# Dense products of a two-block float32 transformer kernel: 512-column matmuls over the high and low parts of x side by side

## The reference

```python
proj = xn @ w_in                                   # 2048 -> 8272
h = h + concat([y_h, y_a]) @ w_out                 # 2048 -> 2048
h = h + square(relu(rms_norm(h) @ w_up)) @ w_down  # 2048 -> 8192 -> 2048
q = rmsnorm(h) @ a_w_in                            # 2048 -> 4096, pooled and gated
h = h + y @ w_out_2                                # twice
```

## Time and profile before

| | |
|---|---|
| median of 3 runs | 2654.34 us (2654.14 to 2654.96) |
| the profiled execution | 2653.12 us |
| its span, first to last instruction | 2651.3 us |
| PE busy | 2428.7 us, 92% |
| POOL busy | 2059.1 us, 78% |
| ACT busy | 1059.0 us, 40% |
| DVE busy | 926.5 us, 35% |
| HBM traffic | 150 GB/s over the span |

### The profile page before, as it was taken

The page is one execution under the profiler, slowest core; times in us unless marked ns, Lnnn a source line. Parts: engine busy times, 40 slices in busy tenths (PEclk is TensorE's granted clock), DMA queues, the critical chain, the costliest instruction groups (busy, mean ns, idle before and its releaser), DMA issues.

```text
span 2651.3 us, 45198 instructions
## 1 busy us (share of the span) xinstructions
PE 2428.7 (92%) x18299; PEld 2322.7 (88%) x18299; DVE 926.5 (35%) x1484; ACT 1059.0 (40%) x1282; POOL 2059.1 (78%) x1956
## 2 busy tenths in 40 slices
PE   6999998868997899999999999998899977999996
PEld 6989997657996799999999999998899956988896
DVE  5026661635252353021031131605514043055522
ACT  3344444474334333333333333433434323244532
POOL 6988984655785679899899999799687958665583
PEclk9999998998998999999999999999999978899998
DMA  5654433332443345555555555454354535433241
GB/s 178 194 169 145 143 105 120 134 140 98 159 159 111 124 137 185 188 177 187 179 182 184 180 185 192 153 187 148 122 187 149 193 109 174 133 110 111 97 157 50
DMA packets 206437, 400.30 MB, mean 151 GB/s; under 512 B 10434, under 2 KB 20932, under 8 KB 205252
## 3 DMA queue, kind: packets, MB, share of 16 engines
q1 hardware_dynamic: 206276, 397.99, 46.1%
HBM read 395.87 MB, written 2.10 MB: 150 GB/s over the span
## 4 chain that ended last, share of the span: by engine, by line
PE 56%; POOL 25%; issue 8%; DVE 6%; ACT 3%; DMA 1%; POOLq 0%; SPq 0%; DVEq 0%; ACTq 0%
PE bank L579 49%; POOL w_low L546 25%; PE bank L696 1%; PE bank L779 1%; PE bank L715 1%; ACT w_high L1035 1%; PE bank L732 1%; PE bank L685 1%; DVE x_low L1473 0%; DVE x_high L1385 0%; DVE x_high L1470 0%; DMA ring<-in_w_in 0%; PE bank L942 0%; DVE heads_scratch L1803 0%; DVE proj L1329 0%
## 5 line engine op out<-in xcount | busy, mean ns | idle before, releaser
L546 POOL TENSOR_TENSOR w_low<-ring,w_high 128x512 fp32r<-128x512 f32 (+3 forms) x1888 | 2049.4, 1117 | 547.9 <-ACT w_high L1035 543.4
L1035 ACT ACTIVATE w_high<-ring 128x1024 fp32r<-128x1024 f32 (+2 forms) x760 | 788.0, 1040 | 1441.8 <-PE bank L579 1414.4
L579 PE MATMUL bank<-x_high,w_high 128*128 128x256 f32 x4196 | 1214.7, 289 | 75.4 <-DVE x_low L1389 21.4
L579 PE MATMUL bank<-x_low,w_high 128*128 128x256 f32 x4196 | 1200.5, 286 | 0.0
L579 PE MATMUL bank<-x_high,w_low 128*128 128x256 f32 x4196 | 1199.8, 286 | 0.0
L579 PEld LDWEIGHTS bank<-x_high,w_high 128*128 128x128 f32 x4196 | 819.8, 195 | 89.0 <-issue 56.3
L579 PEld LDWEIGHTS bank<-x_low,w_high 128*128 128x128 f32 x4196 | 819.8, 195 | 1.6 <-issue 1.4
L579 PEld LDWEIGHTS bank<-x_high,w_low 128*128 128x128 f32 x4196 | 818.8, 195 | 0.0
L579 PE MATMUL bank<-hidden,w_high 128*128 128x256 f32 x2048 | 368.8, 283 | 0.0
L579 PEld LDWEIGHTS bank<-hidden,w_high 128*128 128x128 f32 x2048 | 319.5, 192 | 0.0
L579 PE MATMUL bank<-hidden,w_low 128*128 128x256 f32 x1024 | 289.8, 283 | 0.0
(11 more groups left out here) (250 smaller groups left out, 1667.1 us busy)
## 6 DMA issues: line engine op xcount, KB each, us to landing
ring<-in_w_in SPq DMA_DIRECT2D x64, 1024.0 KB, 5.4
ring<-in_w_up SPq DMA_DIRECT2D x64, 1024.0 KB, 5.3
ring<-in_w_down SPq DMA_DIRECT2D x64, 1024.0 KB, 5.0
ring<-in_w_out SPq DMA_DIRECT2D x48, 1024.0 KB, 5.0
ring<-in_a_w_in SPq DMA_DIRECT2D x32, 1024.0 KB, 5.3
ring<-in_b_w_in SPq DMA_DIRECT2D x32, 1024.0 KB, 5.3
ring<-in_w_kv SPq DMA_DIRECT2D x24, 1024.0 KB, 5.1
ring<-in_w_mem_kv SPq DMA_DIRECT2D x16, 1024.0 KB, 5.0
```

The costliest lines, as they stand in the source:

```text
L546: last = pool.tensor_tensor(w_low[:, u % UNITS, part], ring[:, u // 2, first:first + n], w_high[:, u % UNITS, part], ALU.subtract)
L579: mm = pe.matmul(out, lhs, rhs, start=start and n == 0, stop=stop and n == 2, skip_group_check=True)
L1035: act.activation(w_high[:, u % UNITS, 0:n], ring[:, u // 2, r0 * g.width:r0 * g.width + n], ACT.Copy)\
```

## The change

The dense feature products hgrn_qf, mix_out, up0 to up3, down0 to down3, pool_in, out0 and out1 (4, 4, 32, 6, 4 and 4 blocks, 54 in all) are made in another way. x_high and x_low (and the two parts of hidden) lie side by side for each k tile, 512 columns. PE moves both past one load of w_high, into a bank of its own for each of the 4 feature blocks, and adds w_low times x_high with 256 columns to the first half of the bank. In each k tile the four wide matmuls come first, then the four narrow ones. A group takes four banks, 0 to 3 or 4 to 7. DVE adds the two halves of a bank when it reads it: four instructions for the second halves, a wait, four for the first halves, then the rest. The second halves go to a scratch of their own or to hT. At the first block of a product the norm's sums still use bank 4, so the second block waits for the root. Three products (mix_out, out0, out1) wait for all earlier groups before their first block. cross_out now has a pair of banks for each of its four groups.

```diff
-        x_high = sb("x_high", [P, KT, T], F32R)
-        x_low = sb("x_low", [P, KT, T], F32R)
+        x_split = sb("x_split", [P, KT, 2, T], F32R)
+        x_high, x_low = x_split[:, :, 0, :], x_split[:, :, 1, :]
...
+            def wide_unit(g, b, u, four, x, first, of, more=0):
+                pe.wait_ge(low_ready, 8 * b + u + 1 + more)
+                wh, wl = parts(u, g)
+                r0, rows = g.unit(u)
+                for k in range(rows):
+                    kt = first + r0 + k
+                    for f in range(4):
+                        pe.matmul(four[f][:, :], wh[:, k, f * P:f * P + P], x(kt), start=(kt == 0), stop=False,
+                                  skip_group_check=True)
+                    for f in range(4):
+                        mm = pe.matmul(four[f][:, 0:T], wl[:, k, f * P:f * P + P], x(kt)[:, 0:T], start=False,
+                                       stop=(kt == of - 1), skip_group_check=True)
+                mm.then_inc(units_used, 1)
...
+            def wide_product(name, x, made, ready=x_ready, sums=None):
...
+                        wide_unit(g, g.b0 + n, u, bank[4 * (n % 2):4 * (n % 2) + 4], x, 4 * (u // 2), KT, more)
+                for n in range(2):
+                    if n == 1 and sums:
+                        pe.wait_ge(norm_root, normed[0])
+                    block_of(n, 0, 0, n == 0)
...
+            def second_halves(four, read, out=None):
+                for f in range(4):
+                    b = four[f][:, T:2 * T]
+                    if out is None:
+                        last = dve.tensor_copy(second[:, f * T:f * T + T], b)
+                    else:
+                        last = dve.tensor_tensor(out(f), b, out(f), ALU.add)
+                last.then_inc(halves_read, 1)
+                dve.wait_ge(halves_read, read)
+            def first_halves(four, out=None):
+                for f in range(4):
+                    to = second[:, f * T:f * T + T] if out is None else out(f)
+                    last = dve.tensor_tensor(to, four[f][:, 0:T], to, ALU.add)
+                return last
...
+            def keep_wide(name, t0):
...
+                    second_halves(four, read)
+                    first_halves(four).then_inc(evacuated, 1)
+                    dve.wait_ge(evacuated, i * 2 + (g.g0 + q + 1))
+                    dve.tensor_tensor(proj[:, bass.ds(i * 8 + (t0 + 4 * q), 4), :],
+                                      second.rearrange("p (a t) -> p a t", a=4), scale_four, ALU.mult)\
...
+                def hide(i, q, four, read):
+                    y = second.rearrange("p (a t) -> p a t", a=4)
+                    dve.wait_ge(hidden_ready, i * 2 + (4 * part + q + 1))
+                    second_halves(four, read)
+                    first_halves(four).then_inc(evacuated, 1)
+                    dve.wait_ge(evacuated, i * 2 + (g.g0 + q + 1))
+                    dve.scalar_tensor_tensor(out=y, in0=y, scalar=0.0, in1=scale_four, op0=ALU.max, op1=ALU.mult)\
+                       .then_inc(hidden_squared, 1)
+                    dve.wait_ge(hidden_squared, i * 6 + (12 * part + 3 * q + 1))
+                    dve.tensor_tensor(second, second, second, ALU.mult).then_inc(hidden_squared, 1)
+                    dve.wait_ge(hidden_squared, i * 6 + (12 * part + 3 * q + 2))
+                    high, low = (hidden[:, bass.ds(i * 8 + 4 * q, 4), c, :] for c in range(2))
+                    dve.tensor_copy(high, y).then_inc(hidden_squared, 1)
+                    dve.wait_ge(hidden_squared, i * 6 + (12 * part + 3 * q + 3))
+                    dve.tensor_tensor(low, y, high, ALU.subtract).then_inc(hidden_ready, 1)
```

More of the change, by code:

```diff
@@ L194, in build_program @@
         hidden_squared = sem("hidden_squared")
+        halves_read = sem("halves_read")
+        wide_kept = sem("wide_kept")
         rope_pos = sem("rope_pos")
@@ L612, in pair_of, with block_of @@
                 return bank[2 * (g % 2)], bank[2 * (g % 2) + 1]
+            def wide_product(name, x, made, ready=x_ready, sums=None):
+                g = PLAN[name]
+                def block_of(n, more, more_groups, wait):
+                    group_free(g.g0 + n, more_groups)
+                    for u in range(8):
+                        if wait and u == 6 and sums:
+                            sums()
+                        if wait and u % 2 == 0:
+                            pe.wait_ge(ready, made + u // 2 + 1)
+                        wide_unit(g, g.b0 + n, u, bank[4 * (n % 2):4 * (n % 2) + 4], x, 4 * (u // 2), KT, more)
[3 more added lines that the diff above has]
+                    block_of(n, 0, 0, n == 0)
+                with pe.Fori(0, g.blocks // 2 - 1) as i:
+                    for q in range(2):
+                        block_of(2 + q, i * 16, i * 2, False)
             def product(name, unit, x, made=None, ready=x_ready, sums=None):
@@ L766, in attend @@
                     attend_step(which, which[0] + n)
-            product("hgrn_qf", features_unit, operand, made=x_made["mix"], sums=norm_sum)
+            wide_product("hgrn_qf", operand_parts, x_made["mix"], sums=norm_sum)
             product("hgrn_v", tokens_unit, operand)
@@ L886, in _ @@
             attend(DSA, BESIDE_DSA[LEAD:])
-            product("mix_out", features_unit, operand, made=x_made["mix_y"])
+            pe.wait_ge(evacuated, PLAN["mix_out"].g0)
+            wide_product("mix_out", operand_parts, x_made["mix_y"])
             product("cross_q", features_unit, operand, made=x_made["cross"],
@@ L898, in _ @@
             for u in range(8):
-                if u % 2 == 0:
-                    group_free(g.g0 + u // 2)
-                features_unit(g, g.b0, u, pair_of(g.g0 + u // 2), operand, 0, 4)
+                j = u // 2
+                if u % 2 == 0 and j < 2:
+                    group_free(g.g0 + j)
+                features_unit(g, g.b0, u, bank[2 * j:2 * j + 2], operand, 0, 4)
             for part in range(4):
-                product(f"up{part}", features_unit, operand, made=x_made["mlp"] if part == 0 else None, sums=norm_sum)
-                product(f"down{part}", features_unit, hidden_tile, made=4 * part + 1, ready=hidden_ready)
-            product("pool_in", features_unit, operand, made=x_made["pool"], sums=norm_sum)
+                wide_product(f"up{part}", operand_parts, x_made["mlp"], sums=None if part else norm_sum)
+                wide_product(f"down{part}", hidden_parts, 4 * part + 1, ready=hidden_ready)
+            wide_product("pool_in", operand_parts, x_made["pool"], sums=norm_sum)
             product("pool_qm", features_unit, operand)
@@ L920, in _ @@
                               lambda kt: (x_high[:, 3 * j + kt, :], x_low[:, 3 * j + kt, :]), 0, 3)
-            product("out0", features_unit, operand, made=x_made["pool_y"])
+            pe.wait_ge(evacuated, PLAN["out0"].g0)
+            wide_product("out0", operand_parts, x_made["pool_y"])
             product("cmp_kv", features_unit, operand, made=x_made["kv"], sums=norm_sum)
@@ L997, in _ @@
             attend(range(NSA[0], MEM1[-1] + 1), BESIDE_NSA[ROPED:])
-            product("out1", features_unit, operand, made=x_made["nsa_y"])
+            pe.wait_ge(evacuated, PLAN["out1"].g0)
+            wide_product("out1", operand_parts, x_made["nsa_y"])
             norm_sum()
@@ L1159, in _ @@
             high_parts("hgrn_v")
-            act.wait_ge(evacuated, PLAN["hgrn_v"].g0)
+            act.wait_ge(wide_kept, 4)
             for hg in range(4):
@@ L1231, in _ @@
             high_parts("pool_in", root)
-            act.wait_ge(evacuated, PLAN["pool_qm"].g0)
+            act.wait_ge(wide_kept, 10)
             for t in (12, 16, 20):
@@ L1888, in _ @@
                 then(last)
-                split(blocks, zpe(x_high, c), zpe(x_low, c)).then_inc(x_ready, 1)
+                split(blocks, *(zpe(c, part)[:, 0:n_blocks].rearrange("p (l n) -> p l n", l=CMP_LEN) for part in range(2)))\
+                    .then_inc(x_ready, 1)
             for c, name in enumerate(("cmp_hid_k", "cmp_hid_v")):
```

91 lines of the change are left out of this document (48 added, 43 removed).

## The result

| | before | after |
|---|---|---|
| median of the runs shown with the result | 2653.45 us (2651.21 to 2654.96, 6 runs) | 2668.34 us (2657.80 to 2674.01, 6 runs) |
| ratio, 95% interval | | 1.0054 [1.0031, 1.0077] |
| profiled execution | 2653.12 us, span 2651.3 | 2673.14 us, span 2671.2 |

The predicted time was 2633.5 us with a range of 2626 to 2666: the sign is wrong and the time lies above the range.

The account below looks back on a forecast made before the run. PE was taken as the bound, POOL close behind. 46.0 us saved less 14.5 and 10.5 gives 21.0 off the profiled 2653.12, 2632.1; as median 2633.5 us, 0.8% faster, range 2626 to 2666.

Parts of the forecast that it names:

- 64 fixed costs go, 0.85 us a block, 46.0 us in 54 blocks.: PE's dense products: 64 wide matmuls of 226.7 ns and 64 narrow take 22.19 us a block instead of 23.04.
- a rival of 0.05: PE's wide matmul saves nothing (240 ns or more), only costs are left: 2669 us; chance 0.05.
- the pitch shows nothing: PE: a feature block already changes every third matmul without a trace in the pitch, so 226.7 ns was taken.
- Forecast with its neighbour 0.45: Whole kernel: 2624 to 2640 us, 2633.5 likeliest, together with the case of larger POOL cover; chance 0.45.
- three or four parts 0.33: MLP: DVE shut out by POOL in three or four parts, 2652 to 2667 us; chance 0.33.
- The rival's mechanism: MLP: DVE requests late in a POOL instruction wait for POOL's pause, so PE stops in down for hidden; three or four parts 0.33.
- price of 10.4 us a part: MLP: loss in a part where POOL shuts DVE out, instead of 1.9 to 5; 2664.5 us with all four parts.
- A part's first group is safe: MLP up products: argument for the forecast, against two of four up0 requests having been shut out.
- 4.6 us of cover: MLP up products: how far POOL's w_low may fall behind before PE waits; held enough for the rest.
- the safe phase of 0.19 us: MLP up: squares starting 0.19 us after a POOL instruction took only 2.19 us; today's phase is always that.
- POOL behind in up, 1.9 us a part, 5 in part 0.: Up products: POOL's block of 23.4 us against PE's 22.19 makes PE lose time, 10.5 us in all.
- Ends and first blocks, 14.5 us.: DVE's longer readouts at the ends of mix_out, down3, out0, pool_in, out1, and first blocks of hgrn_qf, up0, pool_in: 14.5 us lost.

Follow-up runs that it names:

- b_fourth: Kernel before, but in the up products two copies read the banks and ReLU and scale follows as a further SBUF instruction; 2667.55 us, ratio 1.0074.

## Why the prediction was wrong

- **"64 fixed costs go, 0.85 us a block, 46.0 us in 54 blocks."** The term that was mis-sized: 0.59 us a block, 31.7 in all, 14.3 less. I carried over 226.7 ns from a product where a wide matmul follows a wide one. Among narrow ones it took 224 to 241 ns, by order. The upper end of 240.0 held the 232 of the changed kernel, but I let it decide only a rival of 0.05 and not the range: 14 us off the gain belong into every case. The argument that "the pitch shows nothing" of a change of feature block was drawn from one order at one width.
- **"Forecast with its neighbour 0.45 ... three or four parts 0.33."** This is the choice that gave the wrong sign: the forecast's sum has PE's wait for `hidden` at nothing, and three fourth groups measured 31.7 us. The rival's mechanism was right in nearly each step: requests passed over until POOL's queue ran dry, little harm in up, PE stopped at unit 6 of down. Its price of 10.4 us a part met the measured 10.55 partly by luck: the wait was 8.96, and the 1.6 us of slow clock behind it were in no sum. Its rule, that a request late in a POOL instruction waits, failed: requests at 1.1 and 1.2 us took 1.2 to 2.4, one at 0.55 took 19.24. With three parts I had 2658; with the 14.3 us of pitch that is 2672, and the profile says 2673.14. What failed is what I set against it. "A part's first group is safe" is true and beside the point, as only the fourth counts. "4.6 us of cover" is about POOL being late for PE, not about DVE getting a turn. And the safe phase of 0.19 us was no safety: b_fourth was shut out at it.
- **"POOL behind in up, 1.9 us a part, 5 in part 0."** Too high: up0 loses 2.5 us and up1 to up3 lose 0.4, 0.7 and 0.7, 4.2 in all for 10.5 (three parts of 1.9 and 5 are 10.7; the sum was out by 0.2). With the 1.9 of down0, where PE waits twice for POOL, it is 6.1. It may be that a shut-out leaves POOL its rhythm and that a stopped PE lets it catch up; that wasn't tried by itself.
- **Ends and first blocks, 14.5 us.** About right in sum. PE's idle time in front of unit 4 of cmp_kv is 5.15 us for 2.79 (5.5 foreseen), the norm's sums after out1 wait 6.73 for 5.15, the first block of pool_in takes 3.4 us more. One item was named wrongly: for pool_zm PE waits 7.67 us for the pooling, less than the 9.04 of the earlier trace rows and not 12 to 13. The time is lost just before, in pool_qm (2.5 us), where PE now waits for POOL four times, 0.8 us each, for two waits of 0.44 and 0.90 before. Beside POOL there DVE scales (1.74 us) and pools in SBUF; no run tells the two apart. In all, the stages outside the MLP are 0.8 us longer: 22 blocks give 12.9 us back and 13.7 are lost. That is net of some 3 us which out0 gains by luck (its first block takes 30.12 us for 33.78; before, a rounding of DVE was shut out there for 6.2 us).
- **The account.** Span +19.9 us = MLP +19.1 (32 blocks, -18.8; three fourth groups +31.7; up products +4.2; down0 +1.9) and the rest +0.8.

From the profile of before, the chance of three or four parts could have been set higher: two of the four squares of up0, where POOL was behind, were passed over for 15.10 and 6.46 us, my own sum had POOL behind in every up product after the change, and the change adds requests to the very row that puts POOL behind. The second median of the changed kernel, 2659.04, and its lowest time, 2651.40, show besides that how many parts are hit is left to chance; the forecast's 2633.5 needs none. A rival whose condition is already in the trace should not weigh less than the forecast that needs it to stay away.

## What to carry to other kernels

When two engines share SBUF and one of them never pauses, count the instructions of the other that must get a turn, not their microseconds: one more a group cost 14 us in the median here, and moving two to a third engine gave 22 to 31 back. Ask of each such instruction who needs its result and when, since shut-outs on results that are wanted late cost 1 to 2 us at most here. Take a matmul's pitch from the order in which it will stand, or keep the difference in the range.

## What the runs showed of the hardware

- A DVE instruction from SBUF to SBUF can be passed over by 16 queued POOL instructions (21.62 us for 1.1 us of work; 14 in the case of 19.24), and it gets in where the next unit's `w_high` comes at most 0.22 us before POOL is done (all 23 waits of over 3 us in six profiles). Readouts from PSUM beside the same queue kept their rhythm, 0.36 us each. The Trainium skill, "SBUF — State Buffer", section "Who interferes with whom", describes the shared ports as an exclusive lock; the trace agrees that one waits for the other, and adds that the lock can go to the same engine again many times over.
- The same wide and narrow matmuls at the granted clock of 1.00, without idle time, gave blocks of 22.19, 22.29, 22.35, 22.45 and 22.61 us by order alone, and one order gave 22.19 or 22.61 without a change in PE's instructions. The cause isn't known; no run here tells banks, weight loads and the other engines' traffic apart.
